# Retention beside the input projections: one block of small matmuls in a unit, both heads side by side, and the bit step ahead of the rotation

## The reference, cut to what matters

```python
scores = jnp.einsum('bnihd,bnjhd->bnhij', q, k) * d_intra
o = jnp.einsum('bnhij,bnjhe->bnihe', scores, v)
u = jnp.einsum('bnjhd,bnjhe->nbhde', k * k_dec[..., None], v)
r_next = g_chunk * r + u                    # state, chunk after chunk
o = o + jnp.einsum('bnihd,nbhde->bnihe', q * q_dec[..., None], r_before)
...
sel_score, sel = lax.top_k(score, n_sel)    # keys of the sparse attention
```

## Time and profile before

| what | value |
|---|---|
| median of three runs | 1665.25 us (1659.36 to 1665.52) |
| the profiled execution | 1659.96 us |
| its span, from first to last instruction | 1658.2 us |
| TensorE, matmul | 1594.6 us busy (96%) |
| VectorE, ScalarE, GpSimd | 795.7, 634.9 and 465.3 us busy |
| mean granted TensorE clock | 0.984 |

### The profile page before, as it was taken

One profiled execution on the slowest core, in us unless ns is written; L12 is line 12 of the kernel. 1 busy time (PEld: TensorE's weight loads), 2 busy tenths in 40 slices (PEclk: granted clock), 3 DMA queues, 4 the chain that ended last, 5 costly groups with the idle time before them and its releaser, 6 DMA issues.

```text
span 1658.2 us, 23346 instructions
## 1 busy us (share of the span) xinstructions
PE 1594.6 (96%) x8496; PEld 1378.1 (83%) x8496; DVE 795.7 (48%) x1557; ACT 634.9 (38%) x1312; POOL 465.3 (28%) x402
## 2 busy tenths in 40 slices
PE   6998999999999799999999999999999999999996
PEld 5985677777777688988889999999898989898985
DVE  4277688878886554423452323232323232323237
ACT  5466576767456676633340212120212120212112
POOL 3211354545441342002331222201222201222206
PEclk9998999999999999999999999999999999999998
DMA  7310311111107352114331111101111101111005
GB/s 215 80 27 20 93 47 36 47 46 35 48 22 153 88 139 55 40 58 151 119 124 51 51 51 51 30 21 51 51 51 51 35 15 51 51 51 51 13 27 203
DMA packets 110673, 107.61 MB, mean 65 GB/s; under 512 B 45529, under 2 KB 93049, under 8 KB 110457
## 3 DMA queue, kind: packets, MB, share of 16 engines
q1 hardware_dynamic: 108816, 105.48, 21.5%
q10 hardware_dynamic: 1768, 1.01, 0.3%
HBM read 87.09 MB, written 19.38 MB: 64 GB/s over the span
## 4 chain that ended last, share of the span: by engine, by line
PE 80%; DVE 4%; ACT 2%; SPq 1%; issue 1%; DMA 1%; POOL 0%; DVEq 0%; ACTq 0%; POOLq 0%
PE paired L381 12%; PE paired L382 12%; PE paired L383 12%; PE wide L381 10%; PE wide L383 10%; PE wide L382 10%; PE paired L1912 4%; PE wide L1885 2%; PE paired L1896 2%; PE wide L1410 1%; PE wide L1404 1%; PE wide L1407 1%; PE wide L1381 1%; PE paired L1871 1%; PE paired L1419 0%
## 5 line engine op out<-in xcount | busy, mean ns | idle before, releaser
L2281 POOL TENSOR_TENSOR aT_lo<-raw_u,aT_hi 128x2048 fp32r<-128x2048 f32 x15 | 69.5, 4633 | 575.8 <-ACT aT_hi L2219 575.8
L2323 DVE CAST fT_hi<-rf 128x768 fp32r<-128x768 f32 x48 | 26.8, 559 | 405.1 <-ACT rf L2232 405.1
L2230 ACT ACTIVATE rf<-paired 128x768 f32<-128x768 f32 x24 | 19.5, 814 | 314.3 <-PE paired L383 314.3
L381 PE MATMUL paired<-w_hi,aT_hi 128*128 128x512 f32 x320 | 137.7, 430 | 1.4 <-PEq L416 1.4
L2230 ACT ACTIVATE rf<-wide 128x768 f32<-128x768 f32 x24 | 19.5, 814 | 307.0 <-PE wide L383 307.0
L382 PE MATMUL paired<-w_lo,aT_hi 128*128 128x512 f32 x320 | 128.1, 400 | 0.0
L383 PE MATMUL paired<-w_hi,aT_lo 128*128 128x512 f32 x320 | 127.8, 399 | 0.0
L383 PE MATMUL wide<-nT_hi,aT_lo 128*128 128x384 f32 x368 | 123.2, 335 | 0.0
L381 PE MATMUL wide<-nT_hi,aT_hi 128*128 128x384 f32 x368 | 123.2, 335 | 0.0
L382 PE MATMUL wide<-nT_lo,aT_hi 128*128 128x384 f32 x368 | 123.1, 334 | 0.0
L383 PE MATMUL paired<-nT_hi,aT_lo 128*128 128x384 f32 x352 | 117.9, 335 | 0.0
(11 more groups left out here) (285 smaller groups left out, 3959.6 us busy)
## 6 DMA issues: line engine op xcount, KB each, us to landing
raw_u<-in_w_up SPq DMA_DIRECT2D x16, 1024.0 KB, 5.6
stage<-in_w_down SPq DMA_DIRECT2D x16, 1024.0 KB, 4.8
stage<-in_w_in SPq DMA_DIRECT2D x32, 256.0 KB, 3.4
stage<-mix_scratch SPq DMA_DIRECT2D x9, 512.0 KB, 4.2
h_scratch<-ob_h SPq DMA_DIRECT2D x9, 512.0 KB, 2.9
stage<-h_scratch SPq DMA_DIRECT2D x9, 512.0 KB, 4.2
out<-acc SPq DMA_DIRECT2D x9, 512.0 KB, 2.9
scores<-in_x_prompt SPq DMA_DIRECT2D x8, 512.0 KB, 5.4
```

The costliest lines, as they stand in the source:

```text
L381: nc.tensor.matmul(out, lhs[0], rhs[0], start=first, stop=False)
L2230: nc.scalar.activation(rf[:, b], up[b][:, :, 0:GT], ACT.Relu).then_inc(relued, 1)
L2281: nc.gpsimd.tensor_tensor(wu[1][:, k], raw_u[:], wu[0][:, k].bitcast(F32), ALU.subtract).then_inc(u_lo, 1)
L2323: nc.vector.tensor_copy(fT[0][:, b], rf[:, b]).then_inc(f_hi, 1)
```

## The change

TensorE's work between the chunks is regrouped. The transposes move from behind chunk 1 to behind chunk 0. `outputs` is taken apart: behind chunk 4 now stand the weighted values of both heads, the state products of both heads (for the sample tile with the streams outside and the heads inside), the scores, and last the state update, all in one block. VectorE settles a bit (and a rank step) ahead of the rotation and not after it, and the last classification of a unit goes behind the scores' decay. The constants are issued in another order, those of the rotation first, with a semaphore of their own.

```diff
     def sync_first(sp):
+        for dst, name in ((cos2, "cos2"), (sin2, "sin2"), (rowdec, "rowdec")):
+            sp.dma_start(dst[:], a[name]).then_inc(rot_in, 16)
         sp.dma_start(goal[:], a["goal"]).then_inc(goal_in, 16)
-        for dst, name in ((cos2, "cos2"), (sin2, "sin2"), (decay, "decay"), (rowdec, "rowdec"),
-                          (carry, "carry"), (own, "own")):
+        for dst, name in ((decay, "decay"), (carry, "carry"), (own, "own")):
             sp.dma_start(dst[:], a[name]).then_inc(const_in, 16)
...
-        pool.wait_ge(const_in, 96)
+        pool.wait_ge(rot_in, 48)
...
                 if pr >= 1:
                     pool.wait_ge(s1_done, pr)
+                else:
+                    pool.wait_ge(const_in, 48)
...
-        dve.wait_ge(const_in, 96)
+        dve.wait_ge(rot_in, 48)
...
+            if r == 0:
+                dve.wait_ge(const_in, 48)
             dve.wait_ge(s_done, r + 1)
...
         for i in range(NT):
-            if 1 <= i <= NR:
-                rotate(i - 1)
             if 1 <= i <= BIT_STEPS:
                 settle_bit(i - 1)
             if i > RANK_FROM:
                 settle_rank(i - RANK_FROM - 1)
+            if 1 <= i <= NR:
+                rotate(i - 1)
...
-            for n in CLASSED.get(i, ()):
+            classes = CLASSED.get(i, ())
+            for n in classes[:-1]:
                 classify(n)
             count(i, 2)
             if 2 <= i < NR + 2:
                 weigh(i - 2)
+            for n in classes[-1:]:
+                classify(n)
             count(i, 3)
...
+        def weighted_values(r):
+            pe.wait_ge(s_dec, r + 1)
+            if r >= 1:
+                pe.wait_ge(ou_done, r)
+            for b in range(2):
+                nc.tensor.matmul(to[:, b, 0:HD], sT[:, r % 2, b], qkvg[:, r % 4, 256 + 64 * b:320 + 64 * b],
+                                 start=True, stop=(unit(r)[1] == 0))
+
+        def from_state(r):
+            pr, t = unit(r)
+            if t == PT:
+                pe.wait_ge(s0_in, 16 * (pr + 1))
+                pe.wait_ge(qm_done, pr + 1)
+                pe.wait_ge(carried, PT * (pr + 1))
+                for s in range(STREAMS):
+                    for b in range(2):
+                        h = slice(64 * b, 64 * b + 64)
+                        nc.tensor.matmul(to[:, b, 0:HD], qm[h, s * P:(s + 1) * P], s0[h, s],
+                                         start=False, stop=(s == STREAMS - 1))
+            elif t >= 1:
+                pe.wait_ge(carried, PT * pr + t)
+                for b in range(2):
+                    h = slice(64 * b, 64 * b + 64)
+                    nc.tensor.matmul(to[:, b, 0:HD], qkT[h, r % 2, 0], state[h, (t - 1) % 2],
+                                     start=False, stop=True)
...
-        def outputs(r):
+        def state_update(r):
             pr, t = unit(r)
-            pe.wait_ge(s_dec, r + 1)
-            if r >= 1:
-                pe.wait_ge(ou_done, r)
...
-                if c == 1 and 2 <= i < NR + 2:
+                if c == 0 and 2 <= i < NR + 2:
                     turn(i - 2)
-                if c == 3 and 3 <= i < NR + 3:
-                    outputs(i - 3)
-                if c == 5 and 2 <= i < NR + 2:
+                if c != 4:
+                    continue
+                if 3 <= i < NR + 3:
+                    weighted_values(i - 3)
+                    from_state(i - 3)
+                if 2 <= i < NR + 2:
                     scores(i - 2)
+                if 3 <= i < NR + 3:
+                    state_update(i - 3)
```

More of the change, by code:

```diff
@@ L924, in retention_programs @@
     ts, to = (x[:].rearrange("p (b n) -> p b n", b=2) for x in wide)
-    const_in, s0_in = sem("rt_const_in"), sem("rt_s0_in")
+    rot_in, const_in, s0_in = sem("rt_rot_in"), sem("rt_const_in"), sem("rt_s0_in")
     proj, evac = sem("rt_proj"), sem("rt_evac")
@@ L1383, in scores @@
             mm.then_inc(s_done, 1)
-        def outputs(r):
+        def state_update(r):
             pr, t = unit(r)
-            pe.wait_ge(s_dec, r + 1)
-            if r >= 1:
-                pe.wait_ge(ou_done, r)
[L1390 to L1393, removed]
+            if t == PT:
                 pe.wait_ge(vm_done, 2 * (pr + 1))
-                pe.wait_ge(carried, PT * (pr + 1))
-            elif t == 0 and pr >= 1:
+            if t == 0 and pr >= 1:
                 pe.wait_ge(s1_done, pr)
[L1398 to L1411, removed]
             for b in range(2):
@@ L1414, in outputs @@
                 k = rotd[:, r % 3, P + 64 * b:P + 64 * b + 64]
-                if sample:
+                if t == PT:
                     mm = nc.tensor.matmul(tu[h, :], k, vm[:, b].rearrange("p s e -> p (s e)"),
```

## The result

| what | before | after |
|---|---|---|
| median | 1665.38 us (1659.36 to 1669.78, 4 runs) | 1623.59 us (1622.44 to 1623.87, 4 runs) |
| profiled span | 1658.2 us | 1622.1 us |
| mean granted TensorE clock | 0.984 | 0.988 |
| VectorE busy | 795.7 us | 757.1 us |

The ratio is 0.9751 [0.9734, 0.9769]: 2.5% faster. The forecast was 1628 with a range of 1616 to 1645.

A forecast was written before the change was run, and what follows sets the result against it. TensorE's own instruction stream was taken as the bound. Savings of 16.3 + 0.4 (first tiles) + 8.8 + 1.6 + 4.2 + 2.4 = 33.7 took 1659.96 to 1626, stated as 1628 us for the gap between runs; range 1616 to 1645.

The forecast's parts named there:

- Plain units: TensorE's units with paired state products and one block: 0.68 us less each (0.43 to 0.78), 16.3 over 24.
- Sample tiles: Four units whose neighbouring sample products lie on different array halves, in one block: 8.8 us saved for the four.
- The clock: TensorE's clock may not fall behind the shortened row in sample units: 1.6 us saved, bounds 0 and 3.2.
- The start and the classes: Earlier rotation constants shorten the third unit by 4.2 us; a classification behind the decay shortens four units by 2.4.
- Bits ahead of the rotation: VectorE's settling fills a wait and makes the rotation about 1.1 us later; costed at nothing.
- The update last in the block: The outputs-ready signal comes some 0.7 us later in its unit; ScalarE's free time covers it, so no cost.
- VectorE as the bound: Rival: VectorE's chain takes 71 to 73 us in nine units, not 69.1; 1634 to 1644 us; chance 0.13.
- Heads one after the other: Rival: the heads' state products don't run side by side, taking away 14 us: 1642; chance 0.08.
- A hidden gain: Rival: ScalarE's and VectorE's bit chain takes 8.1 us a unit whatever TensorE does: 1652 to 1660; chance 0.06.
- a fall of the clock at each block: Rival: behind chunk 4 the clock falls at each combined block, 1.6 us each, 36 times: 1684; chance 0.03.

The follow-up runs named there:

- e3: Changed kernel, but in plain tiles one head's values and state product follow the other's, inside the one block: 1634.34 us, ratio 0.9813.
- e4: Changed kernel, but in sample tiles all eight streams of one head come before those of the other: 1633.18 us, ratio 0.9794.
- e5: Changed kernel with two blocks again: values, state products and update behind chunk 3, scores behind chunk 5: 1632.25 us, ratio 0.9821.
- e1: Kernel before, with only the new order of the constants and their own semaphore: 1662.99 us, ratio 0.9981.
- e2: Kernel before, with only VectorE's order changed, a bit or rank step settled ahead of the rotation: 1662.43 us, ratio 0.9978.
- e6: Changed kernel with the bit and rank steps settled behind the rotation again: 1623.15 us, ratio 0.9763.
- e7: Changed kernel with all classifications ahead of the scores' decay again: 1625.12 us, ratio 0.9780.
- e9: Changed kernel, with SP issuing the bias transfers ahead of the last retention output's store: 1620.47 us, ratio 0.9738.

## Why the prediction was right

**Main mechanism.** TensorE's own stream became shorter, and nothing took the place of the work removed. The predicted sum was 33.7; the stage gave 40.17, of which 38.0 reached the next stage's first product and 36.1 the end of the span. The profiled execution before, 1659.96, less 36.1 is 1623.87; the sum said 1626.

**Plain units.** I took 0.68 with 0.78 as the upper bound; 0.84 was measured. The mis-sized term is the price of the state products. I set all four at the 0.37 of a pair, and kept 0.42 for the scores. They took 0.27 and 0.37. The Trainium skill says in "TensorEngine Tiling (Array Packing)", Tiling Modes, that a change of the array's tiling mode drains TensorE and a change of tile does not. By that rule products before other work of their own shape are cheaper than products before a change; the trace agrees: four instructions took 0.27 before the scores (289.24 to 289.51), and two took 0.36 before 128-row products in e3 (301.65 to 302.01). My bound counted this saving for the scores alone. Over 24 units the error is 0.16 x 24 = 3.8.

**Sample tiles.** Predicted 2.18 for one pair of weighted values and the sample products; measured 2.31 from 250.24 to 252.55 with both pairs, and about 2.07 with one. A unit saved 2.40, against 2.25. E4 shows that 1.39 of it, at the least, is the heads side by side, as even there some of their products overlap; e5 shows 0.35 for the one block.

**The clock.** I counted 1.6, half of two falls; neither came in the sample tiles, so about 3.2. One fall is left in the stage, among the units with the classes, where the granted clock is 0.95. That the length of the row matters is supported by e4, where a row of about 3.4 us (with the two that overlap) brought two falls in four tiles, and in the kernel after 1.8 us brought none. In the kernel before, e1, e2 and e4 the second sample tile met it each time, and one other, the fourth or (in e1) the third. What decides that is open.

**The start and the classes.** 4.2 predicted and 4.2 measured, e1 alone giving it (with the turn a chunk earlier, 0.78 of it needs the bit ahead of the rotation too, as e6 shows). 2.4 predicted, 2.5 measured, e7 giving 2.1 of it back.

**Bits ahead of the rotation** cost nothing, as said; e6 shows that beyond the third unit it also gives nothing. What I had wrong is its effect on VectorE: I left it 67.1 us of chain in the nine units, and it came to 50.76 busy, against 61.99 in e6. That its operations with two inputs fall beside GpSimd's less often is the likely reason, as the gated outputs and the sine products shrank most, but it is not shown: no run takes GpSimd's work away. The units took 67.67, not 69.1, with VectorE at ease.

**The update last in the block** cost nothing either. In the nine units ScalarE waits 12.7 us for it in plain tiles, up to 2.2 at a time, and VectorE 9.2 for ScalarE's counts; TensorE waits for neither. Most of this comes from the bits' order and not from the update's place: in e6, where the update stands as late, ScalarE waits 3.3 and VectorE not at all for counts.

**The step that I left out** is what lies behind the stage. I let all 33.7 reach the end. VectorE's rank steps and SP's queue do not get shorter with TensorE's stream, so 2.17 were lost at once, as e9 shows. That the sum came so near to the time is in part luck: two terms were set too low (plain units and clock, 5.4 together), and what was lost outside the stage (4.1, of which 1.9 are not told from nothing) went the other way.

**The rivals.** VectorE as the bound is refuted by e6: even in the old order it keeps up. Heads one after the other is refuted by the profile, and e3 and e4 show what it would have cost: 10.7 and 9.6 us. A hidden gain and a fall of the clock at each block did not come: nine units at 1.00.

## What to carry to other kernels

When small matmuls use half of TensorE's rows, write the loop so that neighbours lie on different halves, and put groups of the same array shape next to each other: here taking the heads together, with the fewer changes of shape that it brings, was worth about 0.50 us, and joining the blocks 0.34, of an 8.13 us unit. Put the row of small matmuls between projection products and keep it short, and look in the profile whether the clock still falls behind it. Before a gain on the bound engine is booked in full, look at the lists of the other engines and queues that the next stage waits for: what runs there at its own pace takes a part of it back.

## What the runs showed of the hardware that was not expected

TensorE begins an instruction for a free half of the array ahead of one that stands before it in the program: in e3 the first score starts at 302.38 and the last state product at 302.54; in e4 the first score starts at 254.04 and a sample product at 254.14. So its matmuls do not strictly begin in the order of the program.

A VectorE instruction on 128 x 7 elements, 0.17 us elsewhere, took 4.54 us beside GpSimd's second addition (4.61 us), and ended 0.03 us behind it; so it was in the kernel before, and in e9. The Trainium skill says in "SBUF — State Buffer", SBUF: two separate sides, that VectorE and GpSimd share a pair of ports which whoever starts first holds for its whole instruction, and that a VectorE operation with two inputs in SBUF needs it against a GpSimd operation that reads SBUF. The trace agrees: the long instruction reads two tiles, began 0.10 us behind the addition and ended with it.

The mere order of VectorE's list changed its busy time in nine units from 61.99 (e6) to 50.76 us. That this has the same cause is not shown.
